# Feed-forward down products as two row halves side by side, each with a PSUM bank of its own

## The chip, the cores and the metric

The kernel runs on one core of one Trainium2 chip. The metric is the device time of one execution in microseconds (us), lower is better. Before the change it is 2482.23 us, the median of 3 runs (2481.89 to 2484.23).

## The reference

Two transformer blocks in a row, with batch 1 and width 1024. The first has two layers over 256 tokens and 256 context tokens; each layer is a feed-forward, a token mixing (Fourier, neighborhood attention, gated linear attention, grouped attention), an output projection and a second feed-forward, all with modulated RMS norms and gated residuals. The second block has two layers over 272 tokens: forgetting attention and retention, an output projection, a feed-forward. What the change touches is the last product of each of the six feed-forwards:

```python
def swiglu(h, w1, w3, w2):
    return (jax.nn.silu(h @ w1) * (h @ w3)) @ w2      # inner width 2816

# first block, twice a layer:  x = x + gate * swiglu(...)
# second block, once a layer:  h = h + (silu(hn @ w_gate) * (hn @ w_up)) @ w_down
```

## The kernel before

Activations lie transposed: 128 features on the partitions, tokens along the free axis, so that a matmul has 128 rows of weights (the summed features), 128 output features, and 512, 272, 258 or 256 tokens as its columns. float32 accuracy comes from a split: weights and activations are each held as a high part and a low part in the type fp32r, and each product of a 128x128 block of weights is three matmuls, high by high, high by low, low by high (`product`, L726 to L728), which accumulate in one PSUM bank. The weights stream through a ring of three slots ("units", 8 blocks of 128x128 each). For every unit ScalarE writes the high part (`ring_high`, L1177) when TensorE has released the slot, and VectorE then writes the low part (`ring_low`, L1617). TensorE waits for the low part at the first product of a unit (`weights`).

A feed-forward (`ffn`) runs in one or two parts. A part has a gate and an up product for each of its 22 or 11 chunks of the inner width, and then the down products: for each d of 8 chunks of output features, 22 or 11 blocks accumulate in one bank. The banks are taken in turn from 8 (`take`); a bank's next user waits for the VectorE operation that read it. VectorE adds each finished bank to the residual stream (`residual`, its inner `add`, L1783 with a gate, L1781 without). With 512 columns the add is two instructions, one for each stream of tokens.

After the last part comes the norm of the next stage: ScalarE squares the residual chunk (L1198), VectorE sums the squares (L1661), TensorE forms the mean (`mean_square`, L734), ScalarE the inverse root, and VectorE and ScalarE scale and shift each chunk (L1686, L1225) and split it. In the three feed-forwards that end with `late` chunks (both `ffn1` and `ffn2` of layer 0), the last two chunks d are made in two groups of 256 columns (`late_products`), so that the norm of the first group overlaps the second; one `mean_square` stands between their products. In the first parts of two feed-forwards of layer 0 VectorE also makes the dot products of the modulation (`mod_dot`, L1630), interleaved in a fixed order with the splits and the adds.

Every engine works through its instructions in the order of the program; no planner reorders them. `project_out` uses the same names ("down") for its products, with 8 blocks for each d.

Some matmuls of the kernel already have fewer than 128 rows: the attention scores (`scores`, L910 and L918) run on two halves of 64 rows, each in a bank of its own, and the pair products of the linear attention (L970) on four quarters of 32 rows. Their type is plain float32 and not fp32r.

Of the kernel before, what the change touches and what calls it, by code (L numbers as in the profile page):

```python
# [31 lines left out]
ALU = mybir.AluOpType  # L32
# [5 lines left out]
KC = D // P  # L38
# [10 lines left out]
HD = 64  # L49
# [160 lines left out]
def build(nc, A, old=None):  # L210
    ev = Events(*(old or (None, None)))
    ctx = ExitStack()
    with ctx:
# [28 lines left out]
        def when(name, *key):  # L242

            if ev.counting:
                return high_parts, 1
            family, value = ev.known[(name, *key)]
            if family not in ev.sems:
                ev.sems[family] = sem(family)
            return ev.sems[family], value

        def bank(*key):

            return psum[ev.bank_known.get(key, 0)]


        resid = sb("resid", KC * (META + N1)).rearrange("p (c n) -> p c n", c=KC)
# [165 lines left out]
        def chunk(v, c):  # L422
            return v[c] if isinstance(v, list) else v[:, c]
# [277 lines left out]
        def _(pe):  # L701
            taken = [0]
            bank_user = {}

            def take(*key):

                b = taken[0] % 8
                taken[0] += 1
                if b in bank_user:
                    pe.wait_ge(*when("free", *bank_user[b]))  # L710
                bank_user[b] = key
                ev.banks[key] = b
                return psum[b]

            unit = [0]

            def weights():
# [5 lines left out]

            def product(out, w, b, xh, xl, start, stop):

                pe.matmul(out, w[0][:, b], xh, start=start, stop=False)  # L726
                pe.matmul(out, w[0][:, b], xl, start=False, stop=False)  # L727
                return pe.matmul(out, w[1][:, b], xh, start=False, stop=stop)  # L728

            def mean_square(tag, g):  # L730

# [39 lines left out]
            def late_products(tag, h, nb, w, hi, lo, order):  # L771


                late, groups, *_ = after(tag)
                if not late:
                    if not late_scale(tag):
                        mean_square(tag, 0)
                    return
                held = {late[0] * nb // 8: (w, unit[0] - 1)} if late[0] * nb % 8 else {}
                count = 0  # L780
                for g, (a, b, _, _) in enumerate(groups):
                    for d in late:
                        p = take("down", tag, h, d, g)
                        for i in range(nb):
                            j = d * nb + i
                            if j // 8 not in held:
                                held[j // 8] = (weights(), unit[0] - 1)
                            w, u = held[j // 8]
                            f = order[i]
                            mm = product(p[:, 0:b - a], w, f if nb == 8 else j % 8, chunk(hi, f)[:, a:b],  # L790
                                         chunk(lo, f)[:, a:b], i == 0, i == nb - 1)
                            used = u if g == 1 and j % 8 == 7 else None
                            if i == nb - 1:
                                mm.then_inc(*made("down", tag, h, d, g, unit=used))
                            elif used is not None:
                                mm.then_inc(*made("unit_read", used, unit=used))
                            count += 1
                            if count == len(late) * nb + 5:
                                mean_square(tag, 0)
                assert len(held) <= RING  # L800

            def ffn(tag, n, parts, prev):
                xh, xl = parts_for(tag)
                hh, hl = hidden_parts(n, parts)
                cols = SCALED_LATE.get(tag, n)
                nf = FC // parts
                for h in range(parts):
                    for f in range(nf):
                        if h == 0 and f == 0:
                            first_units(tag, [("gate", tag, 0, 0), ("up", tag, 0, 0), ("gate", tag, 0, 1)][:begun(prev)],  # L810
                                        cols, xh, xl, range(KC), prev)
                            continue
                        for what in ("gate", "up")[h == 0 and f == 1 and begun(prev) > 2:]:
                            p = take(what, tag, h, f)
                            w = weights()
                            for c in range(KC):
                                mm = product(p[:, 0:cols], w, c, xh[:, c, 0:cols], xl[:, c, 0:cols],
                                             c == 0, c == KC - 1)
                            mm.then_inc(*made(what, tag, h, f, unit=unit[0] - 1))
                    j = 0  # L820
                    for d in range(first_late(tag) if h == parts - 1 else KC):
                        p = take("down", tag, h, d)
                        for f in range(nf):
                            if j % 8 == 0:
                                w = weights()
                            if d == 0:
                                pe.wait_ge(*when("hidden_low", tag, h, f))
                            mm = product(p[:, 0:n], w, j % 8, hh[:, f], hl[:, f], f == 0, f == nf - 1)
                            j += 1
                            if f < nf - 1 and j % 8 == 0:  # L830
                                mm.then_inc(*made("unit_read", unit[0] - 1, unit=unit[0] - 1))
                        mm.then_inc(*made("down", tag, h, d, unit=unit[0] - 1 if j % 8 == 0 else None))
                    if h == parts - 1:
                        late_products(tag, h, nf, w, hh, hl, range(nf))
# [772 lines left out]
        def _(dve):  # L1607
# [156 lines left out]
            def residual(tag, l, m, streams, h, nb, last_part, dots_of=None):  # L1764
# [8 lines left out]

                def add(d, parts, *g):
                    dve.wait_ge(*when("down", tag, h, d, *g))
                    p = bank("down", tag, h, d, *g)
                    at = parts[0][1]
                    for s, a, b in parts:
                        x = resid[:, d, base + a:base + b]
                        if s is None:  # L1780
                            last = dve.tensor_tensor(x, x, p[:, a - at:b - at], ALU.add)  # L1781
                        else:
                            last = dve.scalar_tensor_tensor(x, p[:, a - at:b - at],  # L1783
                                                            mod[:, l, s, m * KC + d:m * KC + d + 1], x,
                                                            ALU.mult, ALU.add)
                    last.then_inc(*made("resid", tag, h, d, *g, frees=("down", tag, h, d, *g)))

                def add_group(d, g):
# [577 lines left out]
```

## Time and profile before

| | |
|---|---|
| median of 3 runs | 2482.23 us |
| the profiled execution: its time, its span | 2482.26 us, 2480.4 us |
| TensorE busy (matmul / weight load) | 2414.9 us, 97% / 2105.5 us, 85% |
| VectorE, ScalarE, GpSimd busy | 1515.9 us (61%), 1004.3 us (40%), 400.3 us (16%) |
| granted TensorE clock, mean | 0.993 |
| share of TensorE on the chain that ended last | 87% |

A matmul's mean duration in the profile is longer than its turn on the engine, since matmuls overlap; the time from one start to the next is what counts. PE is TensorE's matmul row, PEld its weight loads, DVE VectorE, ACT ScalarE, POOL GpSimd. "L726" is a line of the kernel.

### The profile page before, as it was taken

Reading aid. Unit: us, or ns where it says so; the run is one execution under the profiler, and the core shown is the slowest. Engines: PE = TensorE matmul, PEld = TensorE weight load, DVE = VectorE, ACT = ScalarE, POOL = GpSimd, SP = SyncE. Lnnn points to the kernel's source line nnn. Section 1 sums busy time; section 2 is a strip of 40 time slices with the busy share of each in tenths; the row PEclk is TensorE's granted clock in tenths of the full one; section 3 lists DMA queues with packets and bytes.
Section 4 is the critical chain, followed back from the end, with each engine's and each line's share of the span. In section 5 each row is a group of like instructions: output and inputs, shape, how many; then the busy total and the mean of one; then the engine's idle time right before and its main releaser. Section 6 shows DMA issues by size and latency. Waiting matters only on the chain.

```text
span 2480.4 us, 39346 instructions
## 1 busy us (share of the span) xinstructions
PE 2414.9 (97%) x15046; PEld 2105.5 (85%) x15046; DVE 1515.9 (61%) x2531; ACT 1004.3 (40%) x1651; POOL 400.3 (16%) x410
## 2 busy tenths in 40 slices
PE   7999999999999999999999999999999999999998
PEld 3888888667888888888888877999988999989998
DVE  3878765684599855523323575665666665666664
ACT  4322234554532223422233455545445544445443
POOL 3221211240122122111011131121000120000220
PEclk9999999999999999999999999999999999999999
DMA  7556542212266765222222222455433455434553
GB/s 306 178 199 217 187 161 72 74 52 77 81 211 225 246 217 179 84 103 94 102 94 96 83 77 79 170 180 186 147 110 120 171 177 175 148 111 138 194 187 137
DMA packets 101463, 362.49 MB, mean 146 GB/s; under 512 B 12128, under 2 KB 14304, under 8 KB 101168
## 3 DMA queue, kind: packets, MB, share of 16 engines
q1 hardware_dynamic: 79296, 278.61, 32.3%
q0 software_dynamic: 22000, 81.52, 9.4%
q8 instruction: 120, 1.97, 0.3%
q14 instruction: 47, 0.39, 0.1%
HBM read 359.04 MB, written 1.05 MB: 145 GB/s over the span
## 4 chain that ended last, share of the span: by engine, by line
PE 87%; DVE 5%; ACT 3%; issue 2%; DMA 1%; SPq 0%; POOL 0%; DVEq 0%; ACTq 0%
PE bank L726 27%; PE bank L727 26%; PE bank L728 26%; ACT ring_high L1177 1%; PE bank L948 1%; DVE ring_low L1617 1%; PE bank L918 1%; PE bank L936 1%; DMA small<-small_dram 1%; PE bank L970 1%; DVE arena L1956 1%; PE bank L889 0%; PE bank L1110 0%; DVE arena L1686 0%; PE bank L897 0%
## 5 line engine op out<-in xcount | busy, mean ns | idle before, releaser
L1617 DVE TENSOR_TENSOR ring_low<-ring,ring_high 128x1024 fp32r<-128x1024 f32 x524 | 649.1, 1239 | 558.8 <-ACT ring_high L1177 556.9
L726 PE MATMUL bank<-x_parts,ring_high 128*128 128x512 f32 (+2 forms) x2724 | 922.2, 339 | 14.7 <-DVE ring_low L1617 10.1
L727 PE MATMUL bank<-x_parts,ring_high 128*128 128x512 f32 (+2 forms) x2724 | 904.9, 332 | 0.0
L728 PE MATMUL bank<-x_parts,ring_low 128*128 128x512 f32 (+2 forms) x2724 | 904.5, 332 | 0.0
L1177 ACT ACTIVATE ring_high<-ring 128x1024 fp32r<-128x1024 f32 x524 | 551.6, 1055 | 633.2 <-PE bank L728 631.6
L726 PEld LDWEIGHTS bank<-x_parts,ring_high 128*128 128x128 f32 x2724 | 516.3, 190 | 89.3 <-issue 25.6
L728 PEld LDWEIGHTS bank<-x_parts,ring_low 128*128 128x128 f32 x2724 | 516.1, 189 | 47.3
L727 PEld LDWEIGHTS bank<-x_parts,ring_high 128*128 128x128 f32 x2724 | 515.8, 189 | 46.8 <-issue 0.5
L608 POOL TENSOR_TENSOR hidden_parts<-fresh,hidden_parts 128x512 fp32r<-128x512 f32 (+2 forms) x132 | 216.4, 1640 | 1357.6 <-ACT hidden_parts L1292 1357.6
L726 PE MATMUL bank<-hidden_parts,ring_high 128*128 128x512 f32 (+2 forms) x1122 | 368.0, 328 | 0.9 <-POOL hidden_parts L608 0.9
L728 PE MATMUL bank<-hidden_parts,ring_low 128*128 128x512 f32 (+2 forms) x1122 | 367.3, 327 | 0.0
L727 PE MATMUL bank<-hidden_parts,ring_high 128*128 128x512 f32 (+2 forms) x1122 | 367.2, 327 | 0.0
L1630 DVE CUSTOM_DVE_ANT_0 mod_products<-mod_ring,csilu 128x1024 bf16<-128x1024 f32 x224 | 295.4, 1354 | 53.3 <-DMA mod_ring<-w_mod_dram 52.3
L726 PEld LDWEIGHTS bank<-hidden_parts,ring_high 128*128 128x128 f32 x1122 | 212.7, 190 | 19.5 <-POOL hidden_parts L608 1.3
L727 PEld LDWEIGHTS bank<-hidden_parts,ring_high 128*128 128x128 f32 x1122 | 212.7, 190 | 18.1
L728 PEld LDWEIGHTS bank<-hidden_parts,ring_low 128*128 128x128 f32 x1122 | 212.7, 190 | 18.1
L1283 ACT ACTIVATE act_out<-bank 128x512 f32<-128x512 f32 x66 | 39.5, 598 | 266.8 <-PE bank L728 266.8
L726 PE MATMUL bank<-early_parts,ring_high 128*128 128x258 f32 x352 | 100.0, 284 | 1.5 <-DVE ring_low L1617 1.5
L727 PE MATMUL bank<-early_parts,ring_high 128*128 128x258 f32 x352 | 99.3, 282 | 0.0
L728 PE MATMUL bank<-early_parts,ring_low 128*128 128x258 f32 x352 | 99.3, 282 | 0.0
L1783 DVE SCALAR_TENSOR_TENSOR resid<-bank,mod,resid 128x256 f32<-128x256 f32 x128 | 57.2, 478 | 59.8 <-PE bank L728 59.8
L1198 ACT ACTIVATE squares<-resid 128x256 f32<-128x256 f32 (+2 forms) x86 | 41.2, 481 | 115.3 <-DVE resid L1783 82.6
(217 smaller groups left out, 2189.6 us busy)
## 6 DMA issues: line engine op xcount, KB each, us to landing
ring<-stream_dram SPq DMA_DIRECT2D x524, 512.0 KB, 3.3
mod_ring<-w_mod_dram POOLq DMA_DIRECT2D x128, 512.0 KB, 4.8
arena<-w_mod_first_dram POOLq DMA_DIRECT2D x16, 512.0 KB, 12.0
arena<-na_bias_dram POOLq DMA_DIRECT2D x2, 768.0 KB, 14.0
mod_ring<-consts_dram POOLq DMA_DIRECT2D x1, 1140.0 KB, 5.4
resid<-x_dram SPq DMA_DIRECT2D x1, 1024.0 KB, 10.7
resid<-ctx_dram SPq DMA_DIRECT2D x1, 1024.0 KB, 21.9
csilu<-c_dram POOLq DMA_DIRECT2D x2, 512.0 KB, 9.5
```

The lines of the kernel that those rows point to most:

```text
L608: pool.tensor_tensor(lo[:, f], fresh[:, f % 2, 0:n], hi[:, f].bitcast(F32), ALU.subtract).then_inc(*made("hidden_low", tag, h, f))
L726: pe.matmul(out, w[0][:, b], xh, start=start, stop=False)
L727: pe.matmul(out, w[0][:, b], xl, start=False, stop=False)
L728: return pe.matmul(out, w[1][:, b], xh, start=False, stop=stop)
L918: mm = pe.matmul(out, pr["q"][r, q:q + nq], pr["k"][r, 0:NZ if twin else nk], start=not fox, stop=True, skip_group_check=nq < P)
L936: mm = pe.transpose(p[0:rows, kt * P:kt * P + nq], probs[0:nq, b, e, kt * P:kt * P + rows], cst(C_IDENT, nq, nq))
L1177: act.activation(high[:, u % RING], ring[:, u % RING], ACT.Copy).then_inc(high_parts, 1)
L1198: act.activation(out, resid[:, d, base + a:base + b], ACT.Square).then_inc(*made("resid_squares", tag, d, g))
L1283: act.activation(act_out[:, f % 2, 0:n], p[:, 0:n], ACT.Silu).then_inc(*made("silu", tag, h, f, frees=("gate", tag, h, f)))
L1617: dve.tensor_tensor(low[:, u % RING], ring[:, u % RING], high_f[:, u % RING], ALU.subtract).then_inc(low_parts, 1)
L1630: dve.tensor_tensor_reduce(junk[:, s], mod_ring[:, n % MOD_RING], csilu[:, s], 1.0, 0.0, ALU.mult, ALU.add, mod_raw[:, l, s, j:j + 1]).the ...
L1783: last = dve.scalar_tensor_tensor(x, p[:, a - at:b - at], mod[:, l, s, m * KC + d:m * KC + d + 1], x, ALU.mult, ALU.add)
```

## The change

Each down product of a feed-forward is cut at row 64 of its 128 summed rows. The upper half accumulates in one bank and the lower half in another, so each of the three matmuls of a block becomes two of 64 rows, issued one behind the other, and each d takes two banks of the eight (`take_both`). VectorE adds the first bank to the residual, waits for its own result, and adds the second. The products of `project_out` (8 blocks for each d) stay as they were, and so do all gate, up and projection products.

```diff
+            def take_both(*key):
+                first = take(*key)
+                b = taken[0] % 8
+                taken[0] += 1
+                if b in bank_user:
+                    pe.wait_ge(*when("free", *bank_user[b]))
+                bank_user[b] = key
+                ev.banks[("second", *key)] = b
+                return first, psum[b]
...
             def product(out, w, b, xh, xl, start, stop):
+                if isinstance(out, tuple):
+                    for part, x, first, last in ((w[0], xh, start, False), (w[0], xl, False, False),
+                                                 (w[1], xh, False, stop)):
+                        for e in range(2):
+                            r = slice(HD * e, HD * e + HD)
+                            mm = pe.matmul(out[e], part[r, b], x[r], start=first, stop=last)
+                    return mm
                 pe.matmul(out, w[0][:, b], xh, start=start, stop=False)
...
-                        p = take("down", tag, h, d, g)
+                        p = take_both("down", tag, h, d, g) if nb != 8 else take("down", tag, h, d, g)
...
-                        p = take("down", tag, h, d)
+                        p = take_both("down", tag, h, d)
...
                 def add(d, parts, *g):
                     dve.wait_ge(*when("down", tag, h, d, *g))
-                    p = bank("down", tag, h, d, *g)
+                    two = nb != KC
+                    ps = both_banks("down", tag, h, d, *g) if two else (bank("down", tag, h, d, *g),)
                     at = parts[0][1]
-                    for s, a, b in parts:
...
+                    for i, p in enumerate(ps):
+                        if i:
+                            dve.wait_ge(*when("resid_first", tag, h, d, *g))
+                        for s, a, b in parts:
...
+                        if two and not i:
+                            last.then_inc(*made("resid_first", tag, h, d, *g))
                     last.then_inc(*made("resid", tag, h, d, *g, frees=("down", tag, h, d, *g)))
```

## Rows read from the trace of the kernel before

**Rows 1.** The page: its head and part 1.
```profile
span 2480.4 us, 39346 instructions
...
PE 2414.9 (97%) x15046; PEld 2105.5 (85%) x15046; DVE 1515.9 (61%) x2531; ACT 1004.3 (40%) x1651; POOL 400.3 (16%) x410
```

**Rows 2.** Groups of instructions by form, TensorE: rows*columns of weights, then the moving tile.
```profile
L726 PE MATMUL bank<-hidden_parts,ring_high 128*128 128x512 f32 x462 | 179.9, 389 | 0.9 <-POOL hidden_parts L608 0.9
...
L726 PE MATMUL bank<-hidden_parts,ring_high 128*128 128x256 f32 x484 | 137.5, 284 | 0.0
...
L726 PE MATMUL bank<-hidden_parts,ring_high 128*128 128x272 f32 x176 | 50.7, 288 | 0.0
...
L854 PE MATMUL bank<-const,arena 128*128 128x128 f32 x72 | 12.1, 272 | 0.0
```

**Rows 3.** Busy time by stretch: the nine down stretches, all engines (four of nine, and their sum).
```profile
170.27:230.00 59.73, 59.73 (x265) 49.48 (x264) 53.20 (x88) 12.33 (x12) 9.47 (x16) 1.00 0.69 230
...
785.93:846.90 60.97, 60.06 (x265) 49.41 (x264) 58.44 (x97) 12.21 (x12) 10.96 (x19) 1.00 0.72 253
...
1699.09:1762.44 63.35, 63.35 (x530) 63.35 (x530) 35.20 (x44) 30.13 (x38) 2.28 (x2) 1.00 0.53 183
2061.16:2127.23 66.07, 66.07 (x530) 66.07 (x529) 34.74 (x43) 30.19 (x38) 2.24 (x2) 1.00 0.51 176
...
sum 556.59, PE 555.68 PEld 500.77 DVE 311.70 ACT 182.78 POOL 36.49; mean PE 61.74 PEld 55.64 DVE 34.63 ACT 20.31 POOL 4.05
```

**Rows 4.** Timeline of TensorE: plain float32 matmuls in quarters, whole, halves, whole.
```profile
490.67 0.39 PE L728 MATMUL bank<-x_parts,ring_low 128*128 128x512 f32 x1
490.98 1.17 PE L970 MATMUL bank<-mod_ring 32*128 32x128 f32 x32
...
1478.97 0.28 PE L728 MATMUL bank<-x_parts,ring_low 128*128 128x256 f32 x1
1479.18 0.73 PE L970 MATMUL bank<-mod_ring 32*128 32x128 f32 x16
1479.84 0.38 PE L726 MATMUL bank<-x_parts,ring_high 128*128 128x256 f32 x1
1480.06 0.28 PE L727 MATMUL bank<-x_parts,ring_high 128*128 128x256 f32 x1
...
464.43 0.60 PE L854 MATMUL bank<-const,arena 128*128 128x128 f32 x4
...
2236.36 0.62 PE L918 MATMUL bank<-arena 64*128 64x272 f32 x4
...
1812.24 0.62 PE L1026 MATMUL bank<-arena,mod_ring 128*128 128x272 f32 x2
```

**Rows 5.** Timeline of VectorE late in the down stretch 785.93 to 846.90.
```profile
834.55 2.36 DVE L1617 TENSOR_TENSOR ring_low<-ring,ring_high 128x1024 fp32r<-128x1024 f32 x2
836.82 0.87 DVE L1783 SCALAR_TENSOR_TENSOR resid<-bank,mod,resid 128x256 f32<-128x256 f32 x2
```

**Rows 6.** Timeline around the end of the first feed-forward, VectorE, ScalarE and TensorE.
```profile
403.69 0.43 DVE L1661 TENSOR_TENSOR sumsq<-sumsq,squares 128x256 f32<-128x256 f32 x1 [0.16 <-ACT squares L1198]
...
408.78 0.48 DVE L1783 SCALAR_TENSOR_TENSOR resid<-bank,mod,resid 128x256 f32<-128x256 f32 x1
...
410.70 1.23 DVE L1617 TENSOR_TENSOR ring_low<-ring,ring_high 128x1024 fp32r<-128x1024 f32 x1 [1.44 <-ACT ring_high L1177]
...
409.32 0.40 ACT L1198 ACTIVATE squares<-resid 128x256 f32<-128x256 f32 x1
409.63 1.04 ACT L1177 ACTIVATE ring_high<-ring 128x1024 fp32r<-128x1024 f32 x1
...
404.31 0.59 PE L734 MATMUL bank<-sumsq,const 128*128 128x256 f32 x2
...
412.18 0.36 PE L726 MATMUL bank<-x_parts,ring_high 128*128 128x256 f32 x1 [1.17 <-DVE ring_low L1617]
...
415.05 0.70 PE L734 MATMUL bank<-sumsq,const 128*128 128x256 f32 x2 [0.49 <-DVE sumsq L1661]
```

**Rows 7.** Timeline of TensorE at the end of the last feed-forward.
```profile
2472.44 0.70 PE L734 MATMUL bank<-sumsq,const 128*128 128x256 f32 x2 [1.42 <-DVE sumsq L1661]
```

More of the change, by code:

```diff
@@ L253, in bank, with both_banks @@
             return psum[ev.bank_known.get(key, 0)]
+        def both_banks(*key):
+            return bank(*key), bank("second", *key)
         resid = sb("resid", KC * (META + N1)).rearrange("p (c n) -> p c n", c=KC)
@@ L728, in product, with columns_of @@
                 return pe.matmul(out, w[1][:, b], xh, start=False, stop=stop)
+            def columns_of(p, a, b):
+                return (p[0][:, a:b], p[1][:, a:b]) if isinstance(p, tuple) else p[:, a:b]
             def mean_square(tag, g):
@@ L789, in late_products @@
                             f = order[i]
-                            mm = product(p[:, 0:b - a], w, f if nb == 8 else j % 8, chunk(hi, f)[:, a:b],
+                            mm = product(columns_of(p, 0, b - a), w, f if nb == 8 else j % 8, chunk(hi, f)[:, a:b],
                                          chunk(lo, f)[:, a:b], i == 0, i == nb - 1)
@@ L827, in ffn @@
                                 pe.wait_ge(*when("hidden_low", tag, h, f))
-                            mm = product(p[:, 0:n], w, j % 8, hh[:, f], hl[:, f], f == 0, f == nf - 1)
+                            mm = product(columns_of(p, 0, n), w, j % 8, hh[:, f], hl[:, f], f == 0, f == nf - 1)
                             j += 1
@@ L1775, in add @@
                     dve.wait_ge(*when("down", tag, h, d, *g))
-                    p = bank("down", tag, h, d, *g)
+                    two = nb != KC
+                    ps = both_banks("down", tag, h, d, *g) if two else (bank("down", tag, h, d, *g),)
                     at = parts[0][1]
-                    for s, a, b in parts:
[L1779 to L1785, printed above, removed]
+                    for i, p in enumerate(ps):
+                        if i:
+                            dve.wait_ge(*when("resid_first", tag, h, d, *g))
+                        for s, a, b in parts:
+                            x = resid[:, d, base + a:base + b]
+                            if s is None:
+                                last = dve.tensor_tensor(x, x, p[:, a - at:b - at], ALU.add)
+                            else:
+                                last = dve.scalar_tensor_tensor(x, p[:, a - at:b - at],
+                                                                mod[:, l, s, m * KC + d:m * KC + d + 1], x,
+                                                                ALU.mult, ALU.add)
+                        if two and not i:
+                            last.then_inc(*made("resid_first", tag, h, d, *g))
                     last.then_inc(*made("resid", tag, h, d, *g, frees=("down", tag, h, d, *g)))
```

## The prediction

> **What bounds the kernel now.** I read the page first: TensorE's matmul row is busy for 2414.9 of 2480.4 us, VectorE for 61% [rows 1]. That busy share says only that TensorE has hardly a pause; whether a cheaper or dearer matmul moves the end has to be read from starts. The groups by form count the matmuls that the change touches: a third of them are 462 with 512 columns, 484 with 256 and 176 with 272 [rows 2], and each row has two sisters (L727, L728), so 1386 + 1452 + 528 = 3366. The windows over the nine down stretches give their time: 556.6 us together [rows 3], 22% of the span. The stretch 170.27 to 230.00 holds 264 of them: it ends 0.12 us after the last start, so (59.73 - 0.12) / 263 = 0.2267 us from one start to the next. With 256 columns it is 63.35 / 528 = 0.1200, with 272 columns 66.07 / 528 = 0.1251 [rows 3]. The clock was at its 2.4 GHz level all through (the 1.00 in these rows), where 512 columns stream in 213.3 ns and 256 in 106.7. So each of these matmuls costs its columns and about 13.3 ns more, whatever the columns are. That extra, 3366 x 13.3 = 45 us, is all that a finer cut of the rows can attack: 128 rows already fill the array, and two halves side by side stream each column once, in parallel, just as one matmul of 128 rows does.
>
> TensorE waits for others in few places here. What can bind beside it is VectorE: in the stretch 785.93 to 846.90 it is busy for 58.44 of 60.97 us [rows 3], because the modulation's dot products stand between the splits and the adds.
>
> **The change, part by part.**
>
> *The pairs.* 3366 matmuls go and 3366 pairs come, 64 rows each, in the other half of the array, writing two banks. No fp32r matmul of 64 rows is in the trace. Plain float32 has both kinds. Quarters of 32 rows: 32 of them take 1.17 us and 16 take 0.73, so four groups of four take 0.44, 0.110 us a group; whole matmuls of the same 128 columns take (0.60 - 0.27) / 3 = 0.110, with 0.27 the duration of the last [rows 2, 4]. Halves: two pairs of 272 columns take 0.62, and two whole matmuls of 272 columns take 0.62 as well [rows 4]. So the loads and the matmuls of different row groups do run together, four at a time, and side by side costs the same as whole, to the hundredth. A hundredth over these rows is 2 to 5 ns a group. The pair needs a second issue and cannot be quicker than its slower half; I take 2 ns: 3366 x 0.002 = 6.7 us. The ends that the rows leave are 0 and 5 ns, 0 to 17 us. Nothing in the rows excludes a gain for fp32r, whose 13.3 ns has no counterpart in plain float32 (two whole matmuls of 272 columns are 0.23 apart, hardly over two passes of 113 ns): that is the first rival.
>
> The Trainium skill (TensorE: Matmul & The Clock Gate, Measured speedup vs the span model) adds about 4 ns for each further row tile to a matmul's duration. By that the pairs would cost 13.5 us in place of 6.7. The trace speaks against it in a stream of groups: three such steps are 12 ns, and the quarters' groups are no further apart than whole matmuls are.
>
> *Into and out of the halves.* From a whole matmul of 512 columns to the quarters it takes 0.31 us where its own turn is 0.23, and from 256 columns 0.21 where it is 0.12: 0.09 each. Back, the first whole matmul is 0.22 from the next, where 0.12 is the turn: 0.10, its weight load that could not be taken ahead [rows 4]. I count 0.19 for going in (0.09, and 0.10 for the first load) and 0.2 for coming out. There are nine down stretches, and a `mean_square` of 128 rows inside three of them, so twelve entries: 12 x 0.19 = 2.3. Of twelve exits four end where TensorE waits anyway (the three late ends and the last one, below), so 8 x 0.2 = 1.6. Together 3.9 us; the ends are 2 and 6. The Trainium skill says the same in other words (TensorEngine Tiling (Array Packing), Key Properties: a change of tiling mode drains the engine); the trace agrees, with these 0.09 us.
>
> *VectorE's second add.* Each d now has as many adds again: 0.87 us for the two streams of 512 columns [rows 5], 0.48 for one of 256 [rows 6], and a few hundredths for the wait on its own result; I take 0.90 and 0.51. In six of the nine stretches this is hidden: VectorE is busy for half of them or less. In 170.27 to 230.00 it is busy for 53.20 of 59.73; eight d add 7.2, its idle time is 6.5, and the splits run some 5 us ahead of their use, so I cost it at nothing (up to 2 if that cover is gone).
>
> In 785.93 to 846.90 the cover is not there. VectorE has 2.5 us of idle, nearly all at the start. The unit that TensorE begins after nine units (9 x 24 x 0.2267 = 48.96, plus the 0.9 that it waits for GpSimd, so at 835.8) gets its low part from the first split of the row at 834.55, which ends near 835.75 [rows 5]: it is there just in time. By then five adds have been made, so with the change it is 5 x 0.9 = 4.5 us late and TensorE waits that long for `ring_low`. The adds after it are covered by the later units' slack of some 3 us. I take 4.5; the ends are 3 and 7.
>
> *The late ends.* Three feed-forwards end in a chain of adds. The sum of squares before `mean_square` ends at 404.12 and TensorE takes it at 404.31 [rows 6]: 0.2 of slack against one add of 0.51, so 0.35 late, with the inverse root behind it. Then the add at 408.78 lets ScalarE square the chunk at 409.32; behind that in ScalarE's queue stands the high part at 409.63, then the low part at 410.70, for which TensorE waits until 412.18 [rows 6]: 0.5 more. Then the last add stands ahead of the sum for which `mean_square` waits at 415.05 [rows 6]: 0.5 more. That is 1.35 an end, 4.0 for three; the ends are 2 and 5. At the last feed-forward TensorE waits 1.42 us for the sum [rows 7] and everything behind it is the tail of the kernel: 0.5.
>
> *Banks.* Two of eight for each d; a bank's next user comes four d later, 11 us or more, and the add is done 1 to 5 us after its product. No wait. GpSimd, the DMA queues and the transfers do not change; SP's loads follow the low parts and start later only where those do.
>
> **Sum.** 6.7 + 3.9 + 4.5 + 4.0 + 0.5 = 19.6 us. Against the profiled execution's 2482.26 (its span of 2480.4 and 1.9 around it) that is 2501.9; the median of the runs, 2482.23, is the same execution time to 0.03. I forecast 2502 us, 0.8% slower. The ends of the terms give 0 + 2 + 3 + 2 + 0.5 = 7.5 and 17 + 6 + 7 + 5 + 0.5, with 2 for the first stretch, 37.5; not all fall on one side, so the case's own range is 2491 to 2514.
>
> **Rivals.**
>
> *The extra 13.3 ns goes with half the rows (faster).* If a half pays the few ns of plain float32 instead, a pair takes its streaming time and some 4 ns: 217.3 for 512 columns (9.4 less), 110.7 for 256 (9.3 less), 117.3 for 272 (7.8 less). 1386 x 9.4 + 1452 x 9.3 + 528 x 7.8 = 30.6 us, less 2.5 in the stretch that VectorE bounds. With the 12.9 of the other terms: 15.2 faster, 2467. For it: no other group of the trace pays 13 ns, so it is something special that a cut may escape. Against it: it is the same with 256 and 512 columns, so it belongs to each instruction and not to its loads, and no row shows a half or a quarter quicker than a whole. It wins from a saving of 5.3 ns a pair (12.9 + 5 us, over 3366). The Trainium skill (TensorE: Matmul & The Clock Gate, Wait — 56ns, not 53.3ns?) gives about 2.5 ns as what a back-to-back matmul costs beyond its columns; the trace agrees for plain float32 and not for these. If the halves came down to that, it would be this rival with 1.5 ns more.
>
> *A part of it goes (no change).* With 2.3 to 5.3 ns saved a pair, 8 to 18 us pay for the 12.9: within 0.2%, 2482.
>
> *The change does not do what it says: fp32r halves do not run together.* If the two loads had to follow one another, a pair of 256 or 272 columns would wait for about 0.2 us of loads where it now has 0.12: (1452 + 528) x 0.09 = 180 us, 2680. If the matmuls did, 557 us more. Against it: the 32 quarters in 1.17 us [rows 4], four loads at a time; only the type differs.
>
> **How the numbers follow.** The forecast 0.52, the faster rival 0.34, no change 0.08, the halves apart 0.06. Two runs of this kernel differ by 0.1%, so 0.2% (5 us) is about what a measurement can tell. Faster 0.34, same 0.09 (0.01 from the forecast's lower end), slower 0.57. The range for 8 in 10 takes in the faster rival and the forecast's upper end and leaves out the halves apart: 2463 to 2514.
>
> **What the profile of the changed kernel would show.** The starts in the down stretches: pairs 0.229 us apart with 512 columns and 0.122 with 256 bear me out; 0.217 and 0.111 are the faster rival; 0.2 with 256 columns the halves apart. TensorE's waits for `ring_low` in the stretch from 786: some 4.5 us. The late ends: 1.3 us longer each. An entry of 0.3 us into each stretch. I am wrong if fp32r's extra depends on the rows, which nothing here shows, or if VectorE's lag near 836 costs no time.

## The result, and the profile after

The changed kernel takes 2493.33 us (median of 5 runs, 2492.18 to 2495.14) against 2482.77 of the kernel before beside it (5 runs, 2481.89 to 2484.23): 10.6 us more, a ratio of 1.0042 with a 95% interval of 1.0028 to 1.0057. It is slower, as forecast, but by little more than half of the 19.6 us of the forecast's sum. The profiled execution took 2492.18 us, 9.9 more than that of before; its span is 10.0 longer.

The page of the kernel after, its head and part 1:

```profile
span 2490.4 us, 46273 instructions
...
PE 2419.1 (97%) x18412; PEld 2103.9 (84%) x18412; DVE 1571.6 (63%) x2651; ACT 1005.1 (40%) x1651; POOL 397.4 (16%) x410
```

3366 more matmuls are recorded, 120 more instructions on VectorE with 56 us of work. TensorE's busy time grew by 4 us only; the rest of the 10 is idle time. The product in halves has one line now, so the groups by form hold both halves, and the two matmuls on `ring_high` with them:

```profile
L746 PE MATMUL bank<-hidden_parts,ring_high 64*128 64x512 f32 x1848 | 287.2, 389 | 2.2 <-DVE ring_low L1642 2.1
...
L746 PE MATMUL bank<-hidden_parts,ring_high 64*128 64x256 f32 x1936 | 175.0, 280 | 0.0
...
L746 PE MATMUL bank<-hidden_parts,ring_high 64*128 64x272 f32 x704 | 66.2, 285 | 0.0
```

Whether a pair costs more than a whole matmul is read from starts. The timeline of TensorE in the first down stretch of the kernel after (a row can hold several matmuls, xcount):

```profile
199.66 0.62 PE L746 MATMUL bank<-hidden_parts,ring_high 64*128 64x512 f32 x4
200.11 0.39 PE L746 MATMUL bank<-hidden_parts,ring_low 64*128 64x512 f32 x2
200.34 0.62 PE L746 MATMUL bank<-hidden_parts,ring_high 64*128 64x512 f32 x4
200.79 0.39 PE L746 MATMUL bank<-hidden_parts,ring_low 64*128 64x512 f32 x2
201.02 0.62 PE L746 MATMUL bank<-hidden_parts,ring_high 64*128 64x512 f32 x4
```

Three pairs from 199.66 to 200.34 and three to 201.02: 0.68 / 3 = 0.2267 us a pair, what a whole matmul of 512 columns took [rows 3]. Over whole stretches it is the same. The busy time by stretch of the kernel after (columns as in [rows 3]; five of the nine, and the sum of all nine):

```profile
169.65:229.60 59.95, 59.95 (x529) 49.31 (x528) 57.14 (x100) 12.33 (x12) 8.97 (x15) 1.00 0.68 224
349.66:411.60 61.94, 61.72 (x663) 53.27 (x662) 35.06 (x59) 20.30 (x27) 2.29 (x2) 1.00 0.30 96
788.57:853.25 64.68, 62.50 (x529) 50.33 (x528) 63.39 (x109) 12.32 (x12) 10.14 (x18) 0.97 0.70 236
...
1710.47:1773.90 63.43, 63.43 (x1057) 63.34 (x1056) 38.52 (x51) 30.24 (x38) 2.20 (x2) 1.00 0.57 180
2071.66:2137.80 66.14, 66.14 (x1057) 66.07 (x1056) 37.71 (x50) 30.14 (x38) 2.15 (x2) 1.00 0.55 176
...
sum 563.31, PE 560.48 PEld 501.48 DVE 356.94 ACT 183.18 POOL 34.62; mean PE 62.28 PEld 55.72 DVE 39.66 ACT 20.35 POOL 3.85
```

The first, the fourth and the fifth are within 0.22 us of what they were [rows 3], though VectorE is busy for 3 to 4 us more in each. The second has a `mean_square` in it and grew from 61.01 to 61.85 us from first to last start. The third grew by 3.7 us, and VectorE is busy for all but 1.3 us of it. The turns also give the extra once more: 0.2267 and 0.120 us are 13.3 ns over 512 and 256 columns at 2.4 GHz, but 0.1251 us is 11.8 ns over 272, before and after.

**Into and out of the halves.** TensorE at the start and at the end of the first down stretch, kernel after:

```profile
169.04 0.39 PE L749 MATMUL bank<-x_parts,ring_high 128*128 128x512 f32 x1
169.26 0.39 PE L750 MATMUL bank<-x_parts,ring_low 128*128 128x512 f32 x1
169.58 0.73 PE L746 MATMUL bank<-hidden_parts,ring_high 64*128 64x512 f32 x4
...
229.35 0.39 PE L746 MATMUL bank<-hidden_parts,ring_low 64*128 64x512 f32 x2
229.67 0.50 PE L748 MATMUL bank<-x_parts,ring_high 128*128 128x512 f32 x1
230.00 0.40 PE L749 MATMUL bank<-x_parts,ring_high 128*128 128x512 f32 x1
```

0.32 us into the halves where 0.23 is the turn; 0.32 and 0.33 out of them: 0.09 and 0.20 too much, as worked out from the plain float32 rows [rows 4]. The second pair inside comes 0.1 late too, and some after it by a few nanoseconds each: 0.16 in all.

**The stretch that VectorE bounds.** TensorE, then VectorE in it:

```profile
834.87 0.73 PE L746 MATMUL bank<-hidden_parts,ring_high 64*128 64x512 f32 x4 [2.12 <-DVE ring_low L1642]
...
836.44 0.63 PE L746 MATMUL bank<-hidden_parts,ring_low 64*128 64x512 f32 x2
836.87 1.06 PE L746 MATMUL bank<-hidden_parts,ring_high 64*128 64x512 f32 x4
837.72 0.63 PE L746 MATMUL bank<-hidden_parts,ring_low 64*128 64x512 f32 x2
```

```profile
833.60 1.22 DVE L1642 TENSOR_TENSOR ring_low<-ring,ring_high 128x1024 fp32r<-128x1024 f32 x1
834.74 1.78 DVE L1812 SCALAR_TENSOR_TENSOR resid<-bank,mod,resid 128x256 f32<-128x256 f32 x4
...
841.01 2.36 DVE L1642 TENSOR_TENSOR ring_low<-ring,ring_high 128x1024 fp32r<-128x1024 f32 x2
```

An add of two streams is 1.78 us long where it was 0.87 [rows 5]. The low part that TensorE needs for the unit after eight units is ready at 834.8, and TensorE has waited 2.27 us beyond its turn for it. Behind the wait the granted clock falls: pairs come 0.427 us apart (836.44 to 837.72 is three), and the window over them shows 0.51, the 1.2 GHz level:

```profile
835.70:839.20 3.50, 3.50 (x20) 2.78 (x18) 3.50 (x7) 0.00 (x0) 0.10 (x1) 0.51 0.79 281
```

Eight pairs at that level cost TensorE 1.6 us. By this reading they cost the kernel nothing of their own (no run has the wait without the fall): the next low part comes from the split at 841.01, near 842.2, TensorE waits 0.2 us for it at 842, and without the fall it would have waited that 1.6 longer.

From first to last start the stretch grew by 3.8 us, from 60.85 to 64.62; 0.16 of that belongs to the halves, as in the first stretch, and 3.6 are VectorE's. On TensorE's side they are 2.27 of the first wait, 1.6 and 0.2 up to the second, 0.7 in small gaps, among them 0.19 of a wait for GpSimd, less the 1.2 us that this wait and the start behind it took in the kernel before.

On VectorE's side they are read from its work ahead of these splits, the kernel before and then the kernel after:

```profile
788.43 1.22 DVE L1630 CUSTOM_DVE_ANT_0 mod_products<-mod_ring,csilu 128x1024 bf16<-128x1024 f32 x1 [2.22 <-DMA mod_ring<-w_mod_dram]
...
795.84 1.22 DVE L1617 TENSOR_TENSOR ring_low<-ring,ring_high 128x1024 fp32r<-128x1024 f32 x1
```

```profile
790.30 1.23 DVE L1655 CUSTOM_DVE_ANT_0 mod_products<-mod_ring,csilu 128x1024 bf16<-128x1024 f32 x1 [0.90 <-DMA mod_ring<-w_mod_dram]
...
797.75 1.21 DVE L1642 TENSOR_TENSOR ring_low<-ring,ring_high 128x1024 fp32r<-128x1024 f32 x1
```

From the split at 795.84 to the one at 834.55 [rows 5] it was 38.71 us; the same two, at 797.75 and 841.01, are now 43.26 apart: 4.55 us more, five adds of 0.91. But VectorE had begun this run of work sooner, counted from TensorE's first start of the stretch: 1.80 us behind it (790.30 - 788.50) where it was 2.56 (788.43 - 785.87), with a shorter wait for a transfer. Against TensorE's start the low part of the split at 841.01 is thus 3.8 us later than before.

**The late ends.** TensorE at the end of the first and of the last feed-forward, kernel after; these answer to [rows 6, 7]:

```profile
404.72 0.70 PE L759 MATMUL bank<-sumsq,const 128*128 128x256 f32 x2 [0.22 <-DVE sumsq L1686]
...
413.21 0.36 PE L748 MATMUL bank<-x_parts,ring_high 128*128 128x256 f32 x1 [1.49 <-DVE ring_low L1642]
...
416.37 0.70 PE L759 MATMUL bank<-sumsq,const 128*128 128x256 f32 x2 [0.78 <-DVE sumsq L1686]
...
2482.43 0.70 PE L759 MATMUL bank<-sumsq,const 128*128 128x256 f32 x2 [1.88 <-DVE sumsq L1686]
```

A wait of 0.22 is new, 1.17 became 1.49, 0.49 became 0.78, and 1.42 became 1.88 at the last one.

### The profile page after: what moved, and what is told of

Its sections match the earlier page's. It is cut to its first block, busy times and chain, and to the rows that moved or that the text cites. A ratio compares the mean times of both kernels' runs of the same rounds, so it can differ in the third digit from the quotient of the medians.

```text
span 2490.4 us, 46273 instructions
## 1 busy us (share of the span) xinstructions
PE 2419.1 (97%) x18412; PEld 2103.9 (84%) x18412; DVE 1571.6 (63%) x2651; ACT 1005.1 (40%) x1651; POOL 397.4 (16%) x410
## 4 chain that ended last, share of the span: by engine, by line
PE 85%; DVE 7%; ACT 3%; issue 3%; DMA 1%; SPq 0%; POOL 0%; DVEq 0%; ACTq 0%
PE bank L746 20%; PE bank L748 20%; PE bank L750 19%; PE bank L749 19%; ACT ring_high L1202 1%; DVE ring_low L1642 1%; PE bank L973 1%; PE bank L943 1%; PE bank L961 1%; DMA small<-small_dram 1%; DVE mod_products L1655 1%; DVE arena L1987 1%; DVE resid L1812 1%; PE bank L995 1%; PE bank L914 0%
## 5 line engine op out<-in xcount | busy, mean ns | idle before, releaser
L746 PE MATMUL bank<-hidden_parts,ring_high 64*128 64x256 f32 (+2 forms) x4488 | 528.5, 326 | 2.2 <-DVE ring_low L1642 2.1
L746 PEld LDWEIGHTS bank<-hidden_parts,ring_high 64*128 64x128 f32 x4488 | 380.4, 186 | 43.6 <-DVE ring_low L1642 3.2
L746 PE MATMUL bank<-hidden_parts,ring_low 64*128 64x512 f32 (+2 forms) x2244 | 369.6, 325 | 0.0
L1655 DVE CUSTOM_DVE_ANT_0 mod_products<-mod_ring,csilu 128x1024 bf16<-128x1024 f32 x224 | 301.4, 1382 | 53.6 <-DMA mod_ring<-w_mod_dram 52.3
L746 PEld LDWEIGHTS bank<-hidden_parts,ring_low 64*128 64x128 f32 x2244 | 214.0, 186 | 18.4
L1812 DVE SCALAR_TENSOR_TENSOR resid<-bank,mod,resid 128x256 f32<-128x256 f32 x232 | 103.8, 480 | 56.3 <-PE bank L746 32.9
L588 POOL DMA_DIRECT2D mod_ring<-w_mod_dram x128 | 69.3, 543 | 121.6 <-DVE mod_raw L1655 121.6
L1765 DVE TENSOR_TENSOR fresh<-act_out,bank 128x512 f32<-128x512 f32 x66 | 45.1, 683 | 62.0 <-PE bank L750 62.0
## 6 DMA issues: line engine op xcount, KB each, us to landing
resid<-x_dram SPq DMA_DIRECT2D x1, 1024.0 KB, 10.6
```

Of the source, the lines that this page charges most:

```text
L588: pool.dma_start(mod_ring[:, n % MOD_RING], A["w_mod"][n // (NMOD * KC), n % (NMOD * KC)]).then_inc(*made(f"mod_loaded{n % MOD_RING}", n, ...
L746: mm = pe.matmul(out[e], part[r, b], x[r], start=first, stop=last)
L1655: dve.tensor_tensor_reduce(junk[:, s], mod_ring[:, n % MOD_RING], csilu[:, s], 1.0, 0.0, ALU.mult, ALU.add, mod_raw[:, l, s, j:j + 1]).the ...
L1765: dve.tensor_tensor(fresh[:, g % 2, 0:n], act_out[:, g % 2, 0:n], p[:, 0:n], ALU.mult).then_inc(*made("hidden", tag, h, g, frees=("up", ta ...
L1812: last = dve.scalar_tensor_tensor(x, p[:, a - at:b - at], mod[:, l, s, m * KC + d:m * KC + d + 1], x, ALU.mult, ALU.add)
```

## The experiments

Seven kernels ran, on two occasions, each beside the kernel before. How much a kernel takes over before is told from the ratio, which follows the means of the runs; where the medians say something else, both stand.

**Whole matmuls, but two banks and two adds.** In place of the halves the first and third product of a block go to the one bank and the second to the other. All rows are used at once, and VectorE adds both:

```diff
                 if isinstance(out, tuple):
-                    for part, x, first, last in ((w[0], xh, start, False), (w[0], xl, False, False),
-                                                 (w[1], xh, False, stop)):
-                        for e in range(2):
...
+                    pe.matmul(out[0], w[0][:, b], xh, start=start, stop=False)
+                    pe.matmul(out[1], w[0][:, b], xl, start=start, stop=stop)
+                    return pe.matmul(out[0], w[1][:, b], xh, start=False, stop=stop)
```

> VectorE's part alone: the matmuls of the down products are whole again (128 rows), but the three of a block go to the two banks in turn (first and third into one, second into the other), and VectorE adds both banks as in the changed kernel. Theory A (most of the 10 us is VectorE's second add): the down stretch of the second feed-forward of layer 0 is 3 to 4 us longer than before, each of the three late ends about 1 us longer, the last end 0.4; together 7 us slower than before, 2489 to 2491. Rival B (the loss is in the halves and their entries, VectorE's adds are hidden): within 2 us of before. The alternating banks also try whether the 13.3 ns beyond the columns come from writing one bank again: then the starts of these matmuls would be 216 to 220 ns apart with 512 columns; I expect 227 and 120 as before.

Measured: 2488.2 us (median of 7) against 2480.8 (20 runs), a ratio of 1.0035 (1.0022 to 1.0049): 8.7 us more by the ratio, 7.4 by the medians (two of its runs took 2496). The stretch that VectorE bounds, and the wait in it:

```profile
785.80:850.50 64.70, 62.33 (x265) 50.33 (x264) 63.42 (x109) 12.32 (x12) 10.17 (x18) 0.97 0.69 235
```

```profile
832.12 0.50 PE L742 MATMUL bank<-hidden_parts,ring_high 128*128 128x512 f32 x1 [2.12 <-DVE ring_low L1639]
```

The stretch is as long as with the halves, with the same wait, and the late ends lengthen as well. So these two losses are the second add's. These whole matmuls change bank at two of every three starts, and all their starts are 0.2267 us apart as before: the bank has no part in the 13.3 ns.

**Halves, but only one add.** The converse: TensorE does the pairs, VectorE adds only the upper bank. The lower rows' products are left out of the residual.

```diff
-                    ps = both_banks("down", tag, h, d, *g) if two else (bank("down", tag, h, d, *g),)
+                    two = False
+                    ps = (bank("down", tag, h, d, *g),)
```

> The halves' part alone: the changed kernel, but VectorE adds only the first bank; the sum of the lower rows' products is left out of the residual. Theory A: no wait of TensorE for ring_low in the stretch from 786, late ends as before but for the entries; 12 entries and 8 exits at 0.2 us, 4 us slower than before, 2485 to 2488. Rival B: as slow as the changed kernel, 2492 to 2494. Steady pairs 0.2267 and 0.120 us apart in both.

Measured: 2486.54 us (11 runs), a ratio of 1.0017 (1.0008 to 1.0025), so 4.2 us over before (2 to 6), 5.7 by the medians, where the changed kernel has 10.5. The same stretch, and TensorE's two largest waits of this kernel, then of the kernel after (us in total, times, longest):

```profile
788.70:849.40 60.70, 60.20 (x528) 49.24 (x528) 58.18 (x97) 12.21 (x12) 10.74 (x19) 1.00 0.73 255
```

```profile
PE bank L748 <- DVE ring_low L1642: 11.0, 10, 1.6
PE bank L759 <- DVE sumsq L1686: 8.3, 6, 5.0
```

```profile
PE bank L748 <- DVE ring_low L1642: 12.5, 10, 1.6
PE bank L759 <- DVE sumsq L1686: 10.3, 9, 5.0
```

The stretch is back at 60.7 us. The two waits fall by 1.5 and 2.0 us: that is what the second add costs at the three late ends and at the last one. What is left, 4.2 us by the ratio, goes with the halves themselves.

**Halves everywhere but in the stretch that VectorE bounds.**

```diff
-                        p = take_both("down", tag, h, d)
+                        p = (take if (tag, h) == (("ffn2", 0), 0) else take_both)("down", tag, h, d)
...
-                    two = nb != KC
+                    two = nb != KC and (tag, h) != (("ffn2", 0), 0)
```

> Undo the change in one stretch of nine: the first part of the second feed-forward of layer 0, where VectorE was busy for 58.4 of 61.0 us, has whole products, one bank and one add again. Theory A: 4 us faster than the changed kernel (3.8 of the stretch, 0.3 of its entry and exit), about 2489. Rival C (this stretch is as good as another, a ninth of the 10 us): 1.1 us faster.

Measured: 2487.78 us (7 runs), a ratio of 1.0023 (1.0012 to 1.0034), 5.7 us over before, 7.0 by the medians. That is 4.8 less than with the change everywhere, with an uncertainty of some 4.5 from the two intervals, so the times alone hardly tell the theory's 4 us from the rival's 1.1; the stretch does. The trace has this stretch at 61.07 us from first to last start (64.62 in the changed kernel, 60.85 before).

**One part of the rows alone, and halves in another order.** The down products of several parts compute 64 rows of the 128, or 32, and leave the others out; in two parts the three products of the upper half are issued before the three of the lower.

```diff
+                if isinstance(out, tuple) and form[0] in (64, 32):
+                    r = slice(0, form[0])
+                    pe.matmul(out[0], w[0][r, b], xh[r], start=start, stop=False)
...
+                if isinstance(out, tuple) and form[0] == "in turn":
+                    for e in range(2):
+                        r = slice(HD * e, HD * e + HD)
+                        pe.matmul(out[e], w[0][r, b], xh[r], start=start, stop=False)
...
```

> What the 13.3 ns hang on, by starts in the trace only; parts of the down sums are left out. In five stretches only a part of the rows is multiplied, one matmul where the changed kernel has a pair: rows 0 to 63 (512 columns in the first parts of ffn1 and ffn2 of layer 0, 256 columns in ffn2 of layer 1, 272 columns in ffn of layer 0) or rows 0 to 31 (512 columns, first part of ffn1 of layer 1). In two others (second part of ffn1 of layer 0, ffn of layer 1) each block's three upper halves are issued before its three lower halves. Theory A, the extra belongs to each instruction whatever its rows: 0.2267, 0.120 and 0.125 us from start to start with 64 and with 32 rows. Rival D, it grows with the rows: 0.220 or less with 64 rows, and less again with 32. Halves issued three by three: if a half may run only beside its neighbour in the queue, a block takes up to twice its time; if the queue lets the lower ones start while the upper ones run, as before.

Measured: one run, 2542.23 us. The stretches with 64 rows alone of 512 columns, with 32 rows alone of 512, with 64 alone of 256, and with halves in turn of 256:

```profile
169.78:229.60 59.82, 59.82 (x265) 48.44 (x264) 52.82 (x88) 12.31 (x12) 9.46 (x16) 1.00 0.69 230
...
1157.40:1267.00 109.60, 109.60 (x263) 83.36 (x264) 20.18 (x26) 12.13 (x12) 1.81 (x1) 0.51 0.16 53
1758.80:1822.00 63.20, 63.20 (x528) 63.20 (x528) 35.05 (x44) 30.11 (x38) 2.14 (x2) 1.00 0.53 181
...
2466.70:2530.00 63.30, 63.30 (x1056) 63.30 (x1056) 32.44 (x42) 25.16 (x29) 2.12 (x2) 1.00 0.45 151
```

264 matmuls of 64 rows take what 264 of 128 take, 0.2267 us each; 528 with 256 columns 0.120 each. So fp32r's extra is there in full for half the rows, and the faster rival had nothing to save. With 32 rows the granted clock fell to the 1.2 GHz level some 3 us into the stretch and stayed there to its end (0.51 in the row above), in the one execution that there is, and there a matmul takes 0.4267 us, which is 512 columns at 1.2 GHz and nothing beyond. The Trainium skill (TensorE: Matmul & The Clock Gate, Wait — 56ns, not 53.3ns?) says that the fixed cost of a matmul shows only at the 2.4 GHz level; the trace agrees in that, with 13.3 ns in place of its 2.5.

The halves issued in turn still run side by side, two starts 10 ns apart every 0.120 us, and both of one line of the program, where L753 to L755 are a half's three products in order:

```profile
2480.38 0.29 PE L753 MATMUL bank<-hidden_parts,ring_high 64*128 64x256 f32 x2
2480.50 0.29 PE L754 MATMUL bank<-hidden_parts,ring_high 64*128 64x256 f32 x2
2480.62 0.29 PE L755 MATMUL bank<-hidden_parts,ring_low 64*128 64x256 f32 x2
```

So TensorE had started the lower half's first product before the upper half's second, which stands ahead of it in the program. That an engine works through its instructions in the program's order, as said of the kernel before, does not hold here between the two halves of the array.

**The dot products dealt out anew.** The changed kernel with fewer of the modulation's dot products in the down stretches, and more in the gate and up products ahead of them. Everything is computed.

```diff
+def weight(step):
+    """11 for each chunk of the inner width before this step, 6 for each down product."""
+    down = min(max(step - FC // 2, 0), KC)
+    return 11 * (step - down) + 6 * down
...
-    return range(first + n * step // MOD_STEPS, first + n * (step + 1) // MOD_STEPS)
+    return range(first + n * weight(step) // weight(MOD_STEPS), first + n * weight(step + 1) // weight(MOD_STEPS))
```

> The changed kernel with the modulation's 192 dot products of layer one dealt out anew: a step of the inner width takes 11 shares, a down product 6, in place of equal shares, so that about 22 of VectorE's dot products leave the down stretch that VectorE bounds and go to the gate and up products before it. The result is the same. Theory (the second adds cost time there only because VectorE has no idle left): TensorE's wait of 2.3 us for ring_low is gone, the stretch falls from 64.6 to about 61.9 (its length with the clock at full speed and an entry into the halves), and the kernel takes 3 to 4 us less than the changed kernel, about 7 us more than before. Rival (the length of that stretch comes from the halves themselves, or from the transfers of the ring): it stays near 64.6 and the time near that of the changed kernel. Second rival: the dot products that are moved ahead delay TensorE in the gate and up products, by as much as they free.

Measured: 2487.44 us (11 runs) against 2482.73 (21 runs), a ratio of 1.0021 (1.0012 to 1.0030), 5.2 us over before (4.7 by the medians) where the changed kernel has 10.5. The same stretch, and the one wait in it:

```profile
791.29:852.30 61.01, 60.20 (x529) 49.24 (x528) 58.03 (x99) 12.21 (x12) 8.88 (x15) 1.00 0.65 223
```

```profile
799.16 0.73 PE L752 MATMUL bank<-hidden_parts,ring_high 64*128 64x512 f32 x4 [0.81 <-POOL hidden_parts L618]
```

The wait for `ring_low` is gone with both adds in place, the wait for GpSimd is back, and the stretch is 3.7 us shorter than in the changed kernel. Six dot products fewer do it (27 in this window for 33), not the 22 that I had expected to move. In the first down stretch TensorE now waits 0.6 us for GpSimd, and that stretch is 0.7 us longer (60.49 us from first to last start, 59.77 in the changed kernel); nothing was lost in the gate and up products that the interval could show. The profiled execution is the longest of the eleven (2491.28 us): TensorE was 2 us late by 53 us, at the start of the program, so its span of 2489.5 is not the one to compare.

**The same deal in the kernel before.** The same edit and nothing else, a try at a version faster than both.

> The kernel before with the same new deal of the dot products, and nothing else. Theory: TensorE waits there for GpSimd for 1 us at the start of the same stretch, not for VectorE's adds, so this gives 0 to 1 us (2480 to 2481 by the time of before). Rival: VectorE's full stretch already costs the kernel before more than its one visible wait, and this gives 2 us or more, the first version that is faster than both. Second rival: slower by 1 to 3 us, since VectorE is later with the splits in the gate and up products.

Measured: 2482.83 us (11 runs) against 2482.73, a ratio of 1.0003 (0.9994 to 1.0012): no difference that the interval shows. It excludes a gain of 2 us and leaves room for a small loss. The wait for GpSimd stays:

```profile
794.37 0.50 PE L732 MATMUL bank<-hidden_parts,ring_high 128*128 128x512 f32 x1 [1.14 <-POOL hidden_parts L614]
```

The stretch is no shorter (61.06 us from first to last start, 60.85 before). So VectorE's full stretch cost the kernel before nothing, but was its last reserve.

**Other types.** The kernel before with three parts' down products in bfloat16 or plain float32; the values are then others.

```diff
+            def typed(ap):
+                return ap.bitcast(BF16)[:, 1::2] if form[0] == "bf16" else ap.bitcast(F32)
...
+                if form[0] is not None:
+                    pe.matmul(out, typed(w[0][:, b]), typed(xh), start=start, stop=False)
```

> The kernel before with the down products of three parts in another type, whole matmuls of 128 rows in the same order: bfloat16 (the upper two bytes of each float32, read with a stride) in the first part of the first feed-forward (512 columns) and in the last feed-forward (256 columns), plain float32 in the first part of the third (512 columns). These values are then not those of the reference. If the 13.3 ns beyond the columns belongs to fp32r, bfloat16 starts come 0.216 us apart with 512 columns and 0.109 with 256, and float32 0.43 apart, two passes of 213 ns with 3 ns beyond. If it belongs to this kernel's use of the array (its loads of 128 x 128 weights, its banks), bfloat16 shows 0.2267 and 0.120 again and float32 0.44 or 0.453. In the first case the few nanoseconds of the rows of before that I took for plain float32 are confirmed as a matter of type, and no cut of the rows could have saved them.

Measured: one run, 2643.75 us. The stretches in bfloat16 with 512 columns, plain float32 with 512, bfloat16 with 256:

```profile
171.32:231.10 59.78, 59.78 (x266) 25.66 (x265) 52.86 (x88) 12.26 (x12) 9.50 (x16) 1.00 0.67 231
1153.68:1380.10 226.42, 226.42 (x530) 100.25 (x528) 20.30 (x26) 12.14 (x12) 1.78 (x1) 1.00 0.08 26
2572.64:2632.50 59.86, 59.86 (x529) 50.55 (x528) 29.71 (x35) 25.12 (x29) 2.24 (x2) 1.00 0.48 159
```

Plain float32 runs as two instructions of two passes each: 528 of them from first to last start in 226.17 us, 0.4292 each, which is 2 x 213.3 ns and 2.5 beyond. It loads the same 128 x 128 weights from the same tiles, so neither these loads nor the issue nor the banks make the 13.3 ns by themselves: against plain float32 they go with the type. bfloat16 answers neither of the two expectations: 0.2267 us with 512 columns and 0.1134 with 256, 13.4 and 6.7 ns beyond the columns, a cost that grows with the columns, where that of fp32r does not. Here it was read with a stride of four bytes, which no other row of this case has, so its number says nothing of bfloat16 laid out densely, and does not show that another type of two bytes is free of the extra.

## Why the prediction was right in its sign and too high

- **The pairs: the term that was mis-sized.** I took 2 ns for each, 6.7 us, between 0 and 17; they measured 0. 0.2267, 0.120 and 0.125 us for 512, 256 and 272 columns are the whole matmuls' turns as well, wherever TensorE waits for nothing. The step that failed is "the pair needs a second issue and cannot be quicker than its slower half; I take 2 ns": the second half starts 3 ns behind the first (10 with 272 columns), and the next pair still comes after the turn of one whole matmul, so the second issue costs nothing. The plain float32 rows had said "the same to the hundredth"; a value inside their rounding was taken for a cost. A smaller slip is that the extra is not 13.3 ns with all columns: with 272 it is 11.8. It takes 0.8 us off the 45 that a finer cut could have saved at most, and nothing else. The rule of the Trainium skill (TensorE: Matmul & The Clock Gate, Measured speedup vs the span model) that I weighed there puts some 4 ns on a further row tile; the 3 ns between two halves' starts agree with it for one group by itself (the 10 with 272 columns do not), and a stream of pairs does not pay it.
- **Into and out of the halves: right.** Foreseen 3.9 us. Where VectorE is not in the way a part of 512 columns costs 0.09 at entry, 0.16 inside and 0.20 at exit more than before, 0.45; one of 256 or 272 columns 0.4, the last one 0.2 for want of an exit; a late part 0.44 (with the halves and one add: 0.09 at entry and 0.55 inside, for `mean_square`, and 0.2 back, for the wait for `ring_low` behind it is 0.97 us where it was 1.17). That is 3 x 0.45 + 2 x 0.4 + 0.2 + 3 x 0.44 = 3.7 us, and the kernel with one add measured 4.2 over before (2 to 6).
- **VectorE in the stretch from 786: right in stretch and cause, 3.6 us for 4.5.** From first to last start it took 64.62 us, before 60.85, and 0.16 of the difference belongs to the halves. The lag of VectorE's own work is what I had: five adds, 4.55 us, up to the low part of the unit after nine. The term came out smaller since VectorE had begun 0.8 us sooner against TensorE's start, and since that low part had 0.27 us to spare in the kernel before (49.90 us after the first start, used at 50.17). The 0.8 us was not foreseen, and no run shows what sets it: in the kernel with whole matmuls and two adds VectorE began 1.8 us behind TensorE too, in the kernels without this lag (halves with one add, whole matmuls in this stretch, dot products dealt anew) 2.3 to 2.8. The place within the stretch was off by a unit: TensorE first waits at the unit after eight, whose low part had 1.3 us to spare and is 2.9 later; what is waited there is not waited at the next. The wait for GpSimd, 0.9 us before and 0.19 now, is no part of the difference: what TensorE does not wait for GpSimd it waits for VectorE. The experiments agree on the cause: whole matmuls with two adds have the loss (64.55), halves with one add do not (60.62), and taking dot products away ends it with both adds in place (60.88).
- **The late ends: right, 1.1 us each for 1.35.** Against the kernel with one add the three waits of the first are 0.29, 0.52 and 0.30 longer, where I had 0.35, 0.5 and 0.5. The third is the one that was off. Sum 3.3 for 4.0; the last end 0.46 for 0.5.
- **A wait that no term had.** In the mixing stage of layer 0, near 531 us, TensorE waits 2.31 us for VectorE (L1893) at L973; before it was 1.19 at the same place. All five traces with halves (or 64 rows alone) in the feed-forward ahead of it have 2.3 to 2.6 us there, all four with whole matmuls 1.2, the one with two adds among them. So some 1.1 us go with the halves and not with the adds; how, no run shows.
- **The total.** 0 + 3.7 + 3.6 + 3.3 + 0.5 = 11.1 us, and 12.2 with that wait, where the spans differ by 10.0 and the medians by 10.6. The first down stretch begins 0.6 us sooner than before, at 169.58 for 170.20, and the times from the sixth down stretch to the seventh, the seventh to the eighth and the eighth to the ninth are 1.1 longer, 1.3 shorter and 1.5 shorter beyond the terms: together 2.3 less. Such swings are there without the change as well: in the kernel before with the dot products dealt anew, the same three are 1.3 longer, 1.3 shorter and 1.4 longer than in the kernel before.
- **The rivals.** *The extra goes with half the rows* and *a part of it goes* are refuted by the pairs and by 64 rows alone, at 0.2267 us. *The halves do not run together* is refuted by the same rows. Hidden adds in the six other parts were rightly priced at nothing, the first stretch too (59.77 us with either one add or two).

What stays open: where fp32r's 13.3 ns come from. They do not depend on the rows (64 or 128) or the bank, they are the same with 256 and 512 columns (11.8 with 272), and they are absent at 1.2 GHz and in plain float32; no run went further.

## What to carry to other kernels

Cutting the rows of a matmul that already fills the array bought nothing here, however smoothly the halves ran side by side: a pair took exactly the turn of the whole matmul, and the second bank must be emptied by someone. Before a change gives an engine more work, look for the one stretch where that engine is full, not at its share of the span, and count its lag from where its work in that stretch begins: here 56 us more of VectorE work cost 7.4 us, half of it in one full stretch and half at the ends, and six dot products less in that stretch gave 3.7 us back. Where rows show two forms to be equal, the value to take is zero, and the rounding is for the range.

## What the runs showed of the hardware that was not expected

- An fp32r matmul at 2.4 GHz took 13.3 ns beyond its 512 or 256 columns, with 128 and with 64 rows (11.8 beyond 272); at 1.2 GHz, with 32 rows, nothing beyond them (0.4267 us for 512 columns), and pairs of 64 rows at that level were 0.427 apart too. Plain float32 took 2.5 ns beyond two passes of 512.
- During a stream of 32-row matmuls, with nothing else at their side, the granted clock was 0.51 for 109.6 us, though TensorE was busy throughout; with 64 rows alone it was 1.00. It is one execution.
- Halves issued one after the other, three upper and then three lower, still ran side by side: TensorE lets a matmul of one row group start ahead of earlier ones of the other, in this trace ahead of two that were issued before it.
- A wait of 2.27 us was followed by 3.4 us at the lower clock level, which hid behind VectorE here by the reading above.
